# Row squares and the last block's scaling in halves of 512 columns at four stage changes of a two-block transformer kernel

## The reference

```python
def rms_norm(x, g):
    xf = x.astype(jnp.float32)
    y = xf * lax.rsqrt(jnp.mean(xf * xf, axis=-1, keepdims=True) + EPS)
    return (y * g.astype(jnp.float32)).astype(x.dtype)

x = x + swiglu(rms_norm(x, ffn_norm[0]), ...)
x = x + diff_attention(rms_norm(x, b_norm), k, v, ...)
x = x + swiglu(rms_norm(x, ffn_norm[1]), ...)
return rms_norm(x, final_norm)
```

## Time and profile before

| | |
|---|---|
| median of 3 runs | 2020.95 us (2019.82 to 2025.08) |
| profiled execution: its time | 2019.93 us |
| profiled execution: its span | 2018.2 us |
| mean granted TensorE clock | 0.992 of full |
| busy share of PE, weight load, DVE, ACT, POOL | 96%, 77%, 59%, 48%, 9% |

### The profile page before, as it was taken

The page is one execution under the profiler, slowest core; times in us unless marked ns, Lnnn a source line. Parts: engine busy times, 40 slices in busy tenths (PEclk is TensorE's granted clock), DMA queues, the critical chain, the costliest instruction groups (busy, mean ns, idle before and its releaser), DMA issues.

```text
span 2018.2 us, 22881 instructions
## 1 busy us (share of the span) xinstructions
PE 1944.6 (96%) x8920; PEld 1562.1 (77%) x8920; DVE 1184.1 (59%) x1548; ACT 965.7 (48%) x1469; POOL 186.4 (9%) x250
## 2 busy tenths in 40 slices
PE   4989989999999999999999999999999999999998
PEld 3757758888878888758888888887777778888886
DVE  7766699998989999763543323325345453333323
ACT  3443258888878888744232223224455542222221
POOL 3110111122111110020000000000021100000000
PEclk8999999999999999999999999999999999999999
DMA  8465379999999999951322232222212133323201
GB/s 292 146 214 193 125 248 370 366 377 378 380 363 357 362 373 366 345 169 69 105 84 89 99 105 84 94 94 68 86 59 83 43 115 105 103 85 105 94 32 42
DMA packets 199976, 366.49 MB, mean 182 GB/s; under 512 B 13466, under 2 KB 83879, under 8 KB 199866
## 3 DMA queue, kind: packets, MB, share of 16 engines
q1 hardware_dynamic: 180960, 342.91, 48.4%
q10 hardware_dynamic: 8858, 11.46, 1.7%
q0 software_dynamic: 10048, 10.62, 1.5%
HBM read 365.05 MB, written 24.65 MB: 193 GB/s over the span
## 4 chain that ended last, share of the span: by engine, by line
PE 81%; DVE 7%; DMA 6%; ACT 3%; issue 2%; SPq 1%; POOL 0%; DVEq 0%; POOLq 0%; ACTq 0%
PE ps L263 79%; DMA raw<-in_w_expert_gate 4%; DVE wlo L210 3%; DMA raw<-in_w_in 1%; ACT whi L191 1%; PE ps L2012 1%; PE ps L2039 1%; SPq L919 1%; DMA raw<-in_ada_w 0%; ACT YB L2104 0%; PE ps L2667 0%; DVE XT1l L2095 0%; DVE XT0l L2095 0%; DVE acc L260 0%; ACT XN L703 0%
## 5 line engine op out<-in xcount | busy, mean ns | idle before, releaser
L210 DVE TENSOR_TENSOR wlo<-raw,whi 128x1024 fp32r<-128x1024 f32 (+1 forms) x576 | 674.1, 1215 | 296.7 <-ACT whi L191 294.4
L191 ACT ACTIVATE whi<-raw 128x1024 fp32r<-128x1024 f32 (+1 forms) x576 | 573.5, 1048 | 233.4 <-PE ps L263 196.4
L263 PE MATMUL ps<-hT5h,whi 128*128 128x512 f32 x352 | 137.0, 389 | 0.6 <-DVE hT5l L260 0.6
L263 PE MATMUL ps<-hT3h,whi 128*128 128x512 f32 x352 | 137.0, 389 | 0.6 <-DVE hT3l L260 0.6
L263 PE MATMUL ps<-hT3h,wlo 128*128 128x512 f32 x352 | 137.0, 389 | 0.0
L263 PE MATMUL ps<-hT3l,whi 128*128 128x512 f32 x352 | 137.0, 389 | 0.0
L263 PE MATMUL ps<-hT5h,wlo 128*128 128x512 f32 x352 | 137.0, 389 | 0.0
L263 PE MATMUL ps<-hT5l,whi 128*128 128x512 f32 x352 | 136.9, 389 | 0.0
L2530 DVE TENSOR_TENSOR tmpT<-tmpT,ps 128x512 f32<-128x512 f32 x44 | 30.1, 684 | 139.7 <-PE ps L263 139.7
L263 PE MATMUL ps<-whi,XT1h 128*128 128x512 f32 x256 | 102.8, 401 | 1.5 <-DVE XT1l L2095 1.5
L263 PE MATMUL ps<-whi,XT0h 128*128 128x512 f32 x256 | 102.9, 402 | 1.2 <-DVE XT0l L2095 1.1
(11 more groups left out here) (446 smaller groups left out, 4045.0 us busy)
## 6 DMA issues: line engine op xcount, KB each, us to landing
raw<-in_w_expert_gate SPq DMA_DIRECT2D x64, 1024.0 KB, 7.4
raw<-in_w_expert_up SPq DMA_DIRECT2D x64, 1024.0 KB, 8.1
raw<-in_w_expert_down SPq DMA_DIRECT2D x64, 1024.0 KB, 7.0
raw<-in_ffn_w_gu SPq DMA_DIRECT2D x44, 1024.0 KB, 5.1
raw<-in_ffn_w_down SPq DMA_DIRECT2D x20, 1024.0 KB, 5.0
raw<-in_ada_w SPq DMA_DIRECT2D x24, 512.0 KB, 5.4
raw<-in_w_in SPq DMA_DIRECT2D x8, 1024.0 KB, 6.0
raw<-in_a_w_in SPq DMA_DIRECT2D x8, 1024.0 KB, 10.7
```

The source lines that it names most:

```text
L191: e.activation(hi[:, c], raw[:, c], ACT.Copy).then_inc(self.S("w_hi"), 1)
L210: e.tensor_tensor(lo[:, c], raw[:, c], hi[:, c].bitcast(F32), ALU.subtract).then_inc(self.S("w_lo"), 1)
L263: return e.matmul(o, l, r, start=start, stop=stop, skip_group_check=True)
```

## The change

Norms 4 to 7 are made by halves. ACT squares columns 0 to 511 of all four blocks as soon as half 0 of the last product has been added (sum in column 24 + tb of `small`, semaphore half_sq), and columns 512 to 1023 after half 1 (sum in column tb, semaphore mean_sq). POOL adds eps to the first sum when it is there, then adds the second sum, then takes the power. DVE scales block 3 of norms 4 to 6 in two instructions of 512 columns, with a signal after each (xn_half, xn). PE, at tf2, tf3 and tf4: blocks 0 and 1, kc 0 to 3; claims; blocks 0 and 1, kc 4 to 6; block 2, kc 0 to 6; block 3, kc 0 to 3 after xn_half; block 3, kc 4 to 6 after xn; kc 7. There is no identity product at these three changes. tf1 is as before, and so is normalize_vec for norm 0. Four semaphores of an earlier stage are merged into two (g_shift and e_shift into max_off, g_exp and e_exp into gate_exp; the DVE side, not shown, changes likewise), with the same instructions in the same order.

```diff
@@ -703,6 +703,31 @@
             e.activation(XN[:, tb, :], X[:, tb, :], ACT.Square, scale=D ** -0.5, accum_out=small[:, tb:tb + 1]).then_inc(
                 S("mean_sq"), 1)
+        def half_square_act(e, c, tb, h):
+            hs = slice(h * 512, (h + 1) * 512)
+            at = 24 + tb if h == 0 else tb
+            e.activation(XN[:, tb, hs], X[:, tb, hs], ACT.Square, scale=D ** -0.5, accum_out=small[:, at:at + 1]).then_inc(
+                S("mean_sq") if h == 1 else S("half_sq"), 1)
+        def halves_act(e, c, name0, name1):
+            for h, name in enumerate((name0, name1)):
+                for tb in range(TB):
+                    e.wait_ge(*R.done(*name(tb)))
+                    half_square_act(e, c, tb, h)
+        def halves_pool(e, own, c):
+            for tb in range(TB):
+                out_ = small[:, 8 + tb:9 + tb]
+                e.wait_ge(S("half_sq"), 4 * (c - 4) + tb + 1)
+                e.tensor_scalar(out_, small[:, 24 + tb:25 + tb], EPS, None, ALU.add).then_inc(*own.up())
+                e.wait_ge(S("mean_sq"), 4 * c + tb + 1)
+                e.wait_ge(*own.now())
+                e.tensor_tensor(out_, out_, small[:, tb:tb + 1], ALU.add).then_inc(*own.up())
+                e.wait_ge(*own.now())
+                e.tensor_tensor(out_, out_, epst[:, 1:2], ALU.pow).then_inc(S("rstd"), 1)
         def root_pool(e, own, out_, x, signal):
             e.tensor_scalar(out_, x, EPS, None, ALU.add).then_inc(*own.up())
@@ -717,7 +742,12 @@
         def normalize_vec(e, c, *tbs):
             for tb in tbs or range(TB):
                 e.wait_ge(S("rstd"), 4 * c + tb + 1)
-                e.tensor_scalar(XN[:, tb, :], X[:, tb, :], small[:, 8 + tb:9 + tb], None, ALU.mult).then_inc(S("xn"), 1)
+                if c < 4 or tb < TB - 1:
+                    e.tensor_scalar(XN[:, tb, :], X[:, tb, :], small[:, 8 + tb:9 + tb], None, ALU.mult).then_inc(S("xn"), 1)
+                else:
+                    for h, signal in enumerate(("xn_half", "xn")):
+                        hs = slice(h * 512, (h + 1) * 512)
+                        e.tensor_scalar(XN[:, tb, hs], X[:, tb, hs], small[:, 8 + tb:9 + tb], None, ALU.mult).then_inc(S(signal), 1)
         norm_of = [0, None, 4, 5, 6]
@@ -753,18 +781,33 @@
             def rows(tb):
                 return S("xn"), SECOND[tb] if c == 1 else 4 * norm_of[c] + tb + 1
-            for tb in range(3):
-                e.wait_ge(*rows(tb))
-                if tb == 0 and c not in APART:
-                    idle_pe(e, R.bank(f"tf{c}", 0), 1)
-                turn(tb, range(4))
-            for kc in range(4, 7):
-                R.claim(e, f"tf{c}", kc)
-            idle_pe(e, R.bank(f"tf{c}", 4), 1)
-            for tb in range(3):
-                turn(tb, range(4, 7))
-            e.wait_ge(*rows(3))
-            turn(3, range(7))
+            if c == 1:
+                for tb in range(3):
+                    e.wait_ge(*rows(tb))
+                    if tb == 0:
+                        idle_pe(e, R.bank(f"tf{c}", 0), 1)
+                    turn(tb, range(4))
+                for kc in range(4, 7):
+                    R.claim(e, f"tf{c}", kc)
+                idle_pe(e, R.bank(f"tf{c}", 4), 1)
+                for tb in range(3):
+                    turn(tb, range(4, 7))
+                e.wait_ge(*rows(3))
+                turn(3, range(7))
+            else:
+                for tb in range(2):
+                    e.wait_ge(*rows(tb))
+                    turn(tb, range(4))
+                for kc in range(4, 7):
+                    R.claim(e, f"tf{c}", kc)
+                for tb in range(2):
+                    turn(tb, range(4, 7))
+                e.wait_ge(*rows(2))
+                turn(2, range(7))
+                e.wait_ge(S("xn_half"), norm_of[c] - 3)
+                turn(3, range(4))
+                e.wait_ge(*rows(3))
+                turn(3, range(4, 7))
             R.claim(e, f"tf{c}", 7)
             for tb in range(TB):
                 turn(tb, [7])
@@ -1406,10 +1449,10 @@
             turned(2)
             mean_square(3)
             turned(3)
-            e.wait_ge(S("g_shift"), 1)
-            e.activation(W4[:, :, :], W4[:, :, :], ACT.Exp).then_inc(S("g_exp"), 1)
-            e.wait_ge(S("e_shift"), 1)
-            e.activation(ST_[:, 7, :], ST_[:, 7, :], ACT.Exp).then_inc(S("e_exp"), 1)
+            e.wait_ge(S("max_off"), 1)
+            e.activation(W4[:, :, :], W4[:, :, :], ACT.Exp).then_inc(S("gate_exp"), 1)
+            e.wait_ge(S("max_off"), 2)
+            e.activation(ST_[:, 7, :], ST_[:, 7, :], ACT.Exp).then_inc(S("gate_exp"), 1)
             W.high(e, W.index["eg0"][1] + 1)
         def first_vec(e, own):
@@ -2488,10 +2531,8 @@
                         blocks_pe(e, W.index[f"fd{l}"][nd:nd + 2], f"fd{l}.{f0}.{h}", AT)
                     nd += 2
-        def ffn_act(e, own, l, hT, AT, c, norm, x_ready):
-            for tb in range(TB):
-                e.wait_ge(*x_ready(tb))
-                rms_act(e, norm, tb)
+        def ffn_act(e, own, l, hT, AT, c, norm, name0, name1):
+            halves_act(e, norm, name0, name1)
             features_act(e, c, hT, lambda kc: col("fn", 8 * l + kc))
             ng = nd = 0
             for f0, fn in FG:
@@ -2867,9 +2908,7 @@
             def take(name, i):
                 W.high(e, W.index[name][i] + 1)
-            for tb in range(TB):
-                e.wait_ge(*R.done("fd0.16.1", tb))
-                rms_act(e, 5, tb)
+            halves_act(e, 5, lambda tb: ("fd0.16.0", tb), lambda tb: ("fd0.16.1", tb))
             e.dma_start(tmpT[0][:, 0:256], g["b_lambda_2"][0].rearrange("a d -> (a d)").partition_broadcast(P)).then_inc(S("lam"), 16)
             features_act(e, 3, hT4, None)
             e.wait_ge(S("lam_sum"), 1)
@@ -3126,14 +3165,17 @@
             more_act(e)
             join_act(e, own)
             gmlp_act(e, own)
-            ffn_act(e, own, 0, hT3, AT, 2, 4, lambda tb: R.done("go1", tb))
+            ffn_act(e, own, 0, hT3, AT, 2, 4, lambda tb: ("go0", tb), lambda tb: ("go1", tb))
             attn_act(e, own)
             e.wait_ge(*R.done("as7", 7))
             e.dma_start(GF[:, :], g["final_norm_2"].partition_broadcast(P)).then_inc(S("fgb"), 16)
-            ffn_act(e, own, 1, hT5, AT5, 4, 6, lambda tb: R.done(f"ao1.{tb}"))
+            ffn_act(e, own, 1, hT5, AT5, 4, 6, lambda tb: (f"ao0.{tb}",), lambda tb: (f"ao1.{tb}",))
+            for tb in range(TB):
+                e.wait_ge(*R.done("fd1.16.0", tb))
+                half_square_act(e, 7, tb, 0)
             for tb in range(TB):
                 e.wait_ge(*R.done("fd1.16.1", tb))
-                rms_act(e, 7, tb)
+                half_square_act(e, 7, tb, 1)
                 if tb < TB - 1:
                     e.wait_ge(S("x_last"), tb + 1)
                     e.dma_start(out[0, tb * P:(tb + 1) * P, :], X[:, tb, :]).then_inc(S("out"), 16)
@@ -3170,12 +3212,12 @@
             experts_pool(e, own)
             more_pool(e)
             gmlp_pool(e, own)
-            rms_pool(e, own, 4, 0, 1, 2, 3)
+            halves_pool(e, own, 4)
             distance_pool(e)
-            rms_pool(e, own, 5, 0, 1, 2, 3)
+            halves_pool(e, own, 5)
             attn_pool(e, own)
-            rms_pool(e, own, 6, 0, 1, 2, 3)
-            rms_pool(e, own, 7, 0, 1, 2, 3)
+            halves_pool(e, own, 6)
+            halves_pool(e, own, 7)
```

More of the change, by code:

```diff
@@ L738, in idle_pe @@
                    True, True)
-        APART = (3, 4)
         def late_features_pe(e, c):
@@ L1746, in route_vec @@
             e.tensor_tensor(AA[:, :, :], OH[:, 0, :, :], OH[:, 1, :, :], ALU.add).then_inc(S("chosen"), 1)
-            e.tensor_tensor(W4[:, :, :], gl, bc(sx(0), 4), ALU.subtract).then_inc(S("g_shift"), 1)
-            e.tensor_tensor(sx(7), sx(5), sx(4), ALU.subtract).then_inc(S("e_shift"), 1)
-            e.wait_ge(S("g_exp"), 1)
+            e.tensor_tensor(W4[:, :, :], gl, bc(sx(0), 4), ALU.subtract).then_inc(S("max_off"), 1)
+            e.tensor_tensor(sx(7), sx(5), sx(4), ALU.subtract).then_inc(S("max_off"), 1)
+            e.wait_ge(S("gate_exp"), 1)
             e.tensor_reduce(sx(2), W4[:, :, :], AX, ALU.add).then_inc(*own.up())
@@ L1794, in route_vec @@
                                         ALU.mult).then_inc(S("slot_id"), 1)
-            e.wait_ge(S("e_exp"), 1)
+            e.wait_ge(S("gate_exp"), 2)
             e.tensor_scalar(sx(8), sx(7), 1.0, None, ALU.add).then_inc(*own.up())
```

## The result

Over 22 runs of each kernel the changed kernel took 2017.07 us in the median (2012.07 to 2020.17) and the kernel before 2019.71 us (2014.47 to 2025.08). The ratio is 0.9985, with a 95% interval of 0.9979 to 0.9992: 3.0 us less, between 1.6 and 4.2. That is a real gain and half of the 0.3% that was named as the bound of "no change". The profiled execution took 2015.59 us.

A forecast was written before the change was run, and what follows sets the result against it. TensorE, busy 96%, loses time only waiting at four places, mostly on block 3's strand; savings of 0.75 at tf3 and tf4, 0.88 at tf2 and 0.48 at the end sum to 2.86 us, giving 2018.1, range 2016.6 to 2021.8.

The forecast's parts named there:

- half square and POOL's cheaper step, each of four: At tf2, tf3, tf4 and the end: halved last square saves 0.45 us, POOL adding two columns instead of eps 0.03.
- half scaling, tf3 and tf4: PE released after 512 columns of block 3 instead of 1024; saves 0.27 us each, at least 0.21, at most 0.38.
- half scaling, tf2: Same early release at tf2, where the iota runs beside the scaling; saves 0.26 to 0.54 us, middle 0.40.
- products left out, tf3 and tf4: No gain by itself; keeps PE's strand shorter, since a kept product would eat 0.2 us of the gain.
- products left out, tf2: Two identity products there; keeping them would eat nearly all of the gain forecast at tf2, 0.88 us.
- The row of 612 ns: Profile row for 512 columns out of SBUF, taken for the half square; with 0.10 us of read-out, 0.71 us.
- half of the extra 0.28: At tf2: first half scaling bears between all and none of the iota's extra 0.28 us, ending after 0.77 or 0.49.
- with the product it would be 1398.5 and eat 0.2: At tf3: PE's strand with the identity product ends at 1398.5, against the new release at 1398.3.
- A, the clock: Without identity products PE's clock falls, 1.5 us a fall; one fall 2019.6 (chance 0.13), two or more slower, 2022.6 (0.07).
- 21 early turns: Early in the program, 21 gapless turns at 0.215 us each, said not to bring PE to full speed; counted for the clock rival.
- B, halves that cost more than half: Each half instruction pays its start again and PE's strand ends 0.1 to 0.2 late; gain about 1.5, 2019.4; chance 0.10.
- C, that the change does not do what it says: PE waits for xn after all or first-half squares come late; scaling's share drops out, gain 1.9, 2019.0; chance 0.05.

The follow-up runs named there:

- e2_whole_squares: Changed kernel with the squares of norms 4 to 7 whole again; add-to-matmul lengths 5.67, 5.24, 5.39 us at tf2, tf3, tf4 and 9.61 at the end.
- e3_whole_scaling: Changed kernel with block 3 scaled in one instruction again; lengths 5.46, 5.04, 5.19 us at tf2, tf3, tf4 and 9.14 at the end.
- e1_products: Changed kernel with the identity products put back; lengths 5.74, 4.77, 4.91 us at tf2, tf3, tf4 and 9.14 at the end.
- e4_order_only: Kernel before with the new order of turns and no products, squares and scaling whole; lengths 5.94, 5.50, 5.65 us at tf2, tf3, tf4 and 9.60 at the end.
- e8: Changed kernel with the attention's iota waiting for the last scaling of norm 4; lengths 4.91, 4.76, 4.92 us at tf2, tf3, tf4 and 9.13 at the end.
- e9: Changed kernel with the iota later and block 3 scaled in pieces of 256 and 768 columns; ratio 0.9985 to the kernel before.
- e6_gap_turns: Changed kernel with POOL's wait lengthened by four extra powers and filled with repeated turns; lengths 7.70, 7.28, 7.42 us at tf2, tf3, tf4 and 9.14 at the end.

## Why the prediction was right

**The sum.** Forecast 2.86 us by the terms, with bounds of 2.1 and 3.2; the four lengths give 2.64, the ratio 3.0 (1.6 to 4.2). Term by term:

| term | forecast | measured | by |
|---|---|---|---|
| half square and POOL's cheaper step, each of four | 0.48 | 0.47 | e2_whole_squares |
| half scaling, tf3 and tf4 | 0.27 | 0.27, 0.26 | e3_whole_scaling |
| half scaling, tf2 | 0.40 | 0.26 | e3_whole_scaling |
| products left out, tf3 and tf4 | keeps 0.2 of the gain | 0.00 | e1_products |
| products left out, tf2 | keeps nearly all of the gain | 0.54 of 0.73 | e1_products |
| new order and no products, all else whole | 0 | 0.00 to 0.01 | e4_order_only |

The row of 612 ns was the right one for the square: the changed kernel's halves take 0.62 to 0.63. With the read-out the step went from 1.16 to 0.73, a saving of 0.43 us; the 0.45 of the sum was 0.02 too much, and the estimate of 0.43 that stood beside it was met. POOL's step gave 0.04 in place of 0.03. That what follows a change moves up whole also held: what a change gains is still there at the next one.

**What was mis-sized.** At tf2 the step "half of the extra 0.28" failed. I took the middle between none and all of it, since the iota could lie on either half. It starts 0.07 us before DVE does and lasts 0.56, which takes it to the end of the first half's 0.49, so the first half bears all of it (0.82 to the first turn, 0.54 without the iota). Both numbers stood in the rows. The start of the iota follows POOL's power as DVE's scaling does, and the two move together. That was the lower end of the term, 0.26.

The other is TensorE's own strand, "with the product it would be 1398.5 and eat 0.2": off by the 0.16 us by which a row's recorded end lies behind the next possible start, as shown above. At tf2 "nearly all of it" was 0.54 of 0.73. Neither changed the sum, since the products were left out.

**The rivals.** A, the clock, did not come true. In the six traces without the products and without a longer wait (the changed kernel, e2, e3, e4, e8, e9) it stayed up at all 18 changes, with waits before block 3's turns of up to 1.56 us (tf2 of e4_order_only); it fell with waits of 3.2 to 3.3. Turns in place of the wait held it (e6_gap_turns). The "21 early turns" that the prediction counts for the rival speak against it, since the clock rose while they ran. Its price of 1.5 us was too high for a second reason: where TensorE waits a little later anyway, part of a fall is made up. B, halves that cost more than half, fell with e2 and e3. C, that the change does not do what it says, fell with the timeline of tf3.

**The time.** 2018.1 was forecast from a median of three, 2020.95; over 22 runs each the medians are 2019.71 and 2017.07. The start was 1.24 us too high, and the same 2.86 us off 2019.71 would give 2016.85. The range of 2016.6 to 2021.8 is nearly twice as wide as the effect, so that it holds the result says little; the evidence for the mechanism is in the lengths. The change is 0.15%, within the 0.3% on which the prediction put 0.91.

## What to carry to other kernels

Where one strand of small steps through four engines separates two stages of full TensorE, cut the last row block's work so that only what depends on the last data stays on it: here a sum in two parts bought 0.47 us a time, and a signal after the first columns 0.27. Two strands of nearly equal length have to be shortened together: at tf2 shortening TensorE's alone gave nothing (e4), the other one alone 0.19 us, both 0.73 (e1). Effects of 0.1% are measured as lengths between two events in a trace that bracket the edit, and a change of order on another engine is looked for by what now starts beside the shortened step, as the iota did.

## What was unexpected

**Where the spread is.** The last column of the table runs from 1026.53 to 1032.56 us, 6.0 us, ahead of nearly everything that differs between the kernels, while the two feed-forward pieces repeat to about 0.05 us where the clock does not fall. In these eleven executions nearly all of the spread arises ahead of the four changes. What makes it was not looked into.

**POOL's small additions last as long as DVE's work beside them.** POOL's addition of eps to one column, 0.22 us, in the changed kernel:

```profile
L724 POOL TENSOR_SCALAR small<-small x16: 217/782/1316, 1020.7 to 2003.1; 128x1 f32<-128x1 f32 x16
```

Its median is 0.78 us and the longest 1.32. Ten of the sixteen start 0.05 us after DVE's scaling of 1024 columns (0.75 to 0.78) or its final scaling by the gain (1.28), and end 0.04 to 0.09 us after it; two more, of 0.82 and 1.15 us, lie beside a weight split of DVE. The second sum of the block comes 1.5 us or more after them, except for block 1 at tf2, where 0.15 us were left. So it costs nothing here, but at that place not by much.
